# One core's transformer block in float32: rotary parts packed four heads to a tile, filling projections one unit ahead, and norms kept with tokens on the partitions

## The reference

```python
q_c, kv_c, k_rope, gq, gk, gv, gr, glow, gate_logits = split_columns(h @ w_in)
q = heads(rms_norm(q_c, q_norm_g) @ w_uq, MLA_HEADS)        # 384 -> 8 heads of 64 + 32
kv = heads(rms_norm(kv_c, kv_norm_g) @ w_ukv, MLA_HEADS)    # 256 -> 8 heads of 64 keys, 64 values
q_rope = rope_2d(q_rope, ...)                               # rotation of the 32 rope columns
p = jax.nn.softmax(s.astype(jnp.float32) * MLA_SCALE, axis=-1)
...
y = rms_norm(o, norm_g).reshape(...) * jax.nn.silu(r)       # gated heads: 4 of 128, two directions
```

## Time and profile before

| | us |
|---|---|
| median of 3 runs | 3150.24 (3149.42 to 3150.46) |
| the profiled execution: its time | 3147.42 |
| its span | 3145.4 |
| mean granted clock of TensorE | 0.986 |

### The profile page before, as it was taken

One profiled execution on the slowest core, in us unless ns is written; L12 is line 12 of the kernel. 1 busy time (PEld: TensorE's weight loads), 2 busy tenths in 40 slices (PEclk: granted clock), 3 DMA queues, 4 the chain that ended last, 5 costly groups with the idle time before them and its releaser, 6 DMA issues.

```text
span 3145.4 us, 38638 instructions
## 1 busy us (share of the span) xinstructions
PE 3038.9 (97%) x13632; PEld 2471.6 (79%) x13632; DVE 1431.6 (46%) x1871; ACT 681.5 (22%) x1187; POOL 2066.3 (66%) x2056
## 2 busy tenths in 40 slices
PE   5889999999999999999999999999999999999998
PEld 3767668778887788888888888888888887888886
DVE  7877852276456664222325322255422246542222
ACT  3244651111002542111122111100211115421110
POOL 4622217666666677777767777777777776777774
PEclk8989999999999999999999999999999999999999
DMA  6611112222222232232322222222222322332221
GB/s 257 246 41 37 34 54 94 94 81 99 96 97 91 94 102 99 94 100 94 107 87 90 98 94 100 94 97 97 94 100 94 100 94 94 101 100 95 97 97 67
DMA packets 86026, 306.73 MB, mean 98 GB/s; under 512 B 9552, under 2 KB 10064, under 8 KB 85648
## 3 DMA queue, kind: packets, MB, share of 16 engines
q1 hardware_dynamic: 82512, 297.73, 28.0%
q10 hardware_dynamic: 3392, 7.28, 0.7%
HBM read 302.87 MB, written 2.10 MB: 97 GB/s over the span
## 4 chain that ended last, share of the span: by engine, by line
PE 90%; DVE 7%; ACT 2%; issue 1%; SPq 1%; DMA 1%; DVEq 0%; ACTq 0%
PE acc L1576 85%; PE acc L725 1%; DVE rec_rec_x L1999 1%; PE side L752 1%; DVE ada_more L1152 1%; DMA xc<-in_ctx 1%; SPq L531 1%; PE side L735 0%; PE side L1576 0%; PE acc L647 0%; PE stat L1639 0%; DVE n_scaled L1129 0%; PE acc L632 0%; DVE rec_rec_x L1997 0%; DVE att_stat L1347 0%
## 5 line engine op out<-in xcount | busy, mean ns | idle before, releaser
L1538 POOL TENSOR_TENSOR w_lo<-w_raw,w_hi 128x512 fp32r<-128x512 f32 x513 | 671.8, 1310 | 1011.2 <-PE acc L1576 982.9
L1576 PE MATMUL acc<-h_hi,w_hi 128*128 128x512 f32 x2224 | 876.2, 394 | 28.7 <-ACT gq L868 11.6
L1576 PE MATMUL acc<-h_lo,w_hi 128*128 128x512 f32 x2224 | 868.5, 391 | 0.0
L1576 PE MATMUL acc<-h_hi,w_lo 128*128 128x512 f32 x2224 | 868.4, 390 | 0.0
L1539 POOL TENSOR_TENSOR w_lo<-w_raw,w_hi 128x512 fp32r<-128x512 f32 x513 | 709.4, 1383 | 0.0
L1576 PEld LDWEIGHTS acc<-h_hi,w_hi 128*128 128x128 f32 x2224 | 418.9, 188 | 130.2 <-issue 16.8
L1576 PEld LDWEIGHTS acc<-h_lo,w_hi 128*128 128x128 f32 x2224 | 419.5, 189 | 85.5 <-issue 1.9
L1576 PEld LDWEIGHTS acc<-h_hi,w_lo 128*128 128x128 f32 x2224 | 419.4, 189 | 85.2
L1527 POOL TENSOR_SCALAR w_hi<-w_raw 128x512 fp32r<-128x512 f32 x513 | 403.7, 787 | 37.1 <-DMA w_raw<-in_weights 37.1
L1968 DVE TENSOR_TENSOR x<-acc,x 128x512 f32 (+1 forms) x160 | 110.7, 692 | 661.8 <-PE acc L1576 661.7
L1576 PE MATMUL acc<-mlp_hid_hi,w_hi 128*128 128x512 f32 x1024 | 398.3, 389 | 0.0
(11 more groups left out here) (347 smaller groups left out, 3543.4 us busy)
## 6 DMA issues: line engine op xcount, KB each, us to landing
w_raw<-in_weights SPq DMA_DIRECT2D x513, 512.0 KB, 3.3
ada<-in_ada SPq DMA_DIRECT2D x36, 512.0 KB, 5.7
ada_more<-in_ada SPq DMA_DIRECT2D x10, 512.0 KB, 18.2
x<-in_x ACTq DMA_DIRECT2D x16, 256.0 KB, 6.6
out<-x SPq DMA_DIRECT2D x8, 256.0 KB, 2.2
cvec<-in_cvec ACTq DMA_DIRECT2D x1, 1024.0 KB, 5.8
ada_n<-in_ada SPq DMA_DIRECT2D x2, 512.0 KB, 17.3
xc<-in_ctx SPq DMA_DIRECT2D x1, 1024.0 KB, 16.7
```

Of the source, the lines that this page charges most:

```text
L1538: pool.tensor_tensor(w_lo[:, slot, 0:half], w_raw[:, slot, 0:half], w_hi[:, slot, 0:half].bitcast(F32), ALU.subtract)
L1576: ins = pe.matmul(out, lhs, rhs, start=start, stop=stop, skip_group_check=group)
```

## The change

- GLA_FILL and gla_order: k of head 1 is projected before unit 0; every later k and q moves one unit forward; unit 5 has no filling projection. gla_output is now an entry of the order.
- Low-rank norms: the sums of squares are products of 24 tiles of low_square (as stationary operand) with one column of ones, so tokens lie on the partitions and a sum is one column. ACT's roots and DVE's reciprocal work on 128x4 and 128x10. The query norm is not applied to z_q: it goes into the softmax scale (score_scale), which exps and probs read as a column instead of a constant. The key norm is spread back over the partitions by ACT (six scaled copies of the identity, key_diagonal) and PE (keys: a ones product of 512 and 256 columns), and DVE scales z_kv by it (low_rank_keys) after the last unit.
- Gated heads: sum is four products of one column; DVE inverts 128x4 (head_inverses); ACT makes four scaled copies of the identity (head_diagonal); PE's new output spread multiplies them by ones; head_output reads that bank. head_output stands one unit later than before.
- Query projections: the rope columns of four heads share a tile, so two outputs hold the rope rows and two their partners, then four outputs hold the 64 plain rows of two heads each. DVE turns a group of four heads with three 128x512 operations. ACT copies the turned rows of heads 0 to 3 into q_t, DVE those of heads 4 to 7. A table rope_q (512 KB) is loaded by a DMA that ACT issues after unit 7.

```diff
-GLA_FILL = [("k", 1, 2), ("q", 1, 1), ("k", 2, 2), ("q", 2, 1), ("k", 3, 2), ("q", 3, 1), ("r", 2, 1), ("r", 3, 1)]
+GLA_FILL = [("q", 1, 1), ("k", 2, 2), ("q", 2, 1), ("k", 3, 2), ("q", 3, 1), None, ("r", 2, 1), ("r", 3, 1)]
 def gla_order():
-    order = [("gate", 0, 2), ("k", 0, 2), ("gate", 1, 2)]
+    order = [("gate", 0, 2), ("k", 0, 2), ("gate", 1, 2), ("k", 1, 2)]
     for u in range(GLA_STEPS):
         order += [("turned", u, 2), ("intra", u, 1), ("added", u, 1)]
         if u % 2 == 0 and u:
             order.append(("sum", u // 2 - 1, 1))
+        if u % 2 == 1 and u > 1:
+            order.append(("spread", u // 2 - 1, 1))
+        if u == GLA_STEPS - 1:
+            order.append(("keys", 0, 2))
         if u + 2 < GLA_STEPS:
             order.append(("gate", u + 2, 2))
-        order.append(GLA_FILL[u])
+        if GLA_FILL[u]:
+            order.append(GLA_FILL[u])
+        order.append(("output", u, 0))
...
+        key_spread = norms[:, 3:5, :].rearrange("p n t -> p (n t)")
+        q_rope = [square[:, 0, :], rstd]
...
+            def token_sums(tiles, n, at):
+
                 out = begin_out()
+                for b in range(n):
+                    for k in range(tiles):
+                        ins = pe.matmul(out[:, b:b + 1], low_square[:, at(k, b):at(k, b) + P], ones[:, 0:1],
+                                        start=(k == 0), stop=(k == tiles - 1))
                 ins.then_inc(out_made, 1)
+            token_sums(QL, 4, lambda k, b: T * k + P * b)
+            token_sums(KVL, 4, lambda k, b: QL * T + TC * k + P * b)
+            token_sums(KVL, KB - 4, lambda k, b: QL * T + TC * k + T + P * b)
...
                 if name == "sum":
                     pe.wait_ge(gla_sq, i + 1)
                     out = begin_out()
+                    for b in range(4):
+                        ins = pe.matmul(out[:, b:b + 1], square[:, i % 2, P * b:P * b + P], ones[:, 0:1], start=True, stop=True)
+                    ins.then_inc(out_made, 1)
+                if name == "spread":
+                    pe.wait_ge(head_diag, i + 1)
+                    out = begin_out()
                     pe.matmul(out[:, :], ones[:, :], square[:, i % 2, :], start=True, stop=True).then_inc(out_made, 1)
+                if name == "keys":
+                    pe.wait_ge(key_diag, 1)
+                    for c0, c1 in ((0, T), (T, TC)):
+                        out = begin_out()
+                        pe.matmul(out[:, 0:c1 - c0], ones[:, :], key_spread[:, c0:c1], start=True, stop=True)\
+                          .then_inc(out_made, 1)
...
+            gla_part("spread", GH - 1)
             slot, _ = next_tile()
...
             def head_root(h):
-                if h:
-                    act.wait_ge(gla_y, h)
-                take(OUT_GLA["sum", h], root[:, :], func=ACT.Sqrt, bias=col("eps"), scale=1.0 / P)
+                take(OUT_GLA["sum", h], head_rstd[:, 0, :], func=ACT.Sqrt, bias=col("eps"), scale=1.0 / P, width=4)
                 load_exp_ln()
+            def head_diagonal(h):
+
+                act.wait_ge(head_inverse, h + 1)
+                for b in range(4):
+                    ins = act.activation(square[:, h % 2, P * b:P * b + P], identity[:, :], ACT.Copy, scale=head_rstd[:, 1, b:b + 1])
+                ins.then_inc(head_diag, 1)
+            def key_diagonal():
+                act.wait_ge(low_inverse, 1)
+                for b in range(KB):
+                    ins = act.activation(key_spread[:, P * b:P * b + P], identity[:, :], ACT.Copy, scale=low_rstd[:, 4 + b:5 + b])
+                ins.then_inc(key_diag, 1)
...
+                if d == 0 and h:
+                    head_diagonal(h - 1)
+                if u == GLA_STEPS - 2:
+                    key_diagonal()
+                    for k in range(QL):
+                        act.activation(zq_hi[k], z_q[:, k, :], ACT.Copy, scale=col("q_norm", k)).then_inc(lr_hi, 1)
                 if d == 1 and h:
                     head_output_high(h - 1)
-                if u == GLA_STEPS - 2:
-                    act.wait_ge(lr_scaled, 2)
-                    for k in range(QL):
-                        act.activation(zq_hi[k], z_q[:, k, :], ACT.Copy).then_inc(lr_hi, 1)
+            wait_taken(act, OUT_GLA["intra", GLA_STEPS - 1])
+            act.dma_start(rope_q[:, :, :], io["rope_q"]).then_inc(rope_in, 16)
...
-            for h in range(HEADS):
-                wait_made(act, OUT_QH + h)
-                act.activation(q_t[0:64, h, :], bank(OUT_QH + h)[0:64, :], ACT.Copy).then_inc(q_copied, 1)
+            for half in range(2):
+                for pair in (2 * half, 2 * half + 1):
+                    o = OUT_QH + 4 + pair
+                    wait_made(act, o)
+                    act.activation(q_t[0:64, 2 * pair, :], bank(o)[0:64, :], ACT.Copy)
+                    act.activation(q_t[0:64, 2 * pair + 1, :], bank(o)[64:P, :], ACT.Copy).then_inc(out_taken[o % BANKS], 1)
+                if half == 0:
+                    act.wait_ge(q_turned, 1)
+                    for j in range(4):
+                        act.activation(q_t[64:96, j, :], q_rope[0][32 * j:32 * j + 32, :], ACT.Copy)
             head_root(GH - 1)
...
+            head_diagonal(GH - 1)
             for tb in range(KB):
                 take(OUT_V + tb, v_mla[:, tb, :])
...
-                    act.activation(prob[:, u % 2, c0:c1], bank(o + i)[:, 0:c1 - c0], ACT.Exp, scale=MLA_SCALE,
+                    act.activation(prob[:, u % 2, c0:c1], bank(o + i)[:, 0:c1 - c0], ACT.Exp, scale=score_scale[:, 0, qb:qb + 1],
...
-                link(dve.reciprocal(square[:, 0, :], square[:, 0, :]))
-                link(dve.reciprocal(square[:, 1, 0:C], square[:, 1, 0:C]))
...
+                own(dve.reciprocal(low_rstd[:, :], low_rstd[:, :]), low_inverse, 1)
+                dve.tensor_scalar(score_scale[:, 0, :], low_rstd[:, 0:4], MLA_SCALE, None, ALU.mult)
+                link(dve.tensor_scalar(score_scale[:, 1, :], low_rstd[:, 0:4], -MLA_SCALE, None, ALU.mult))
...
+            def head_inverses(h):
+
+                wait_taken(dve, OUT_GLA["sum", h])
+                if h:
+                    dve.wait_ge(head_diag, h)
+                own(dve.reciprocal(head_rstd[:, 1, :], head_rstd[:, 0, :]), head_inverse, h + 1)
...
+                take(dve.scalar_tensor_tensor(out=o_norm[:, :], in0=gr[:, h % 2, :], scalar=col("gla_norm"),
+                                              in1=bank(o), op0=ALU.mult, op1=ALU.mult), o)
+                own(dve.tensor_tensor(o_norm[:, :], side[:, h % 2, :], o_norm[:, :], ALU.mult), gla_y, h + 1)
...
-                link(dve.tensor_tensor(square[64:96, 0, :], b[96:P, :], rope[96:P, :], ALU.mult))
-                link(dve.tensor_tensor(q_t[64:96, h, :], b[64:96, :], rope[64:96, :], ALU.mult))
-                dve.wait_ge(q_copied, h + 1)
-                take(dve.tensor_tensor(q_t[64:96, h, :], q_t[64:96, h, :], square[64:96, 0, :], ALU.add), o)
-            wait_made(dve, OUT_KH - 1)
+                take(dve.tensor_tensor(turned, bank(o), rope_q[:, 0, :], ALU.mult), o)
+                wait_made(dve, o + 1)
+                take(dve.tensor_tensor(square_sum[:, :], bank(o + 1), rope_q[:, 1, :], ALU.mult), o + 1)
+                own(dve.tensor_tensor(turned, turned, square_sum[:, :], ALU.add), q_turned, group + 1)
+            wait_made(dve, OUT_QH + HEADS - 1)
+            for j in range(4):
+                dve.tensor_copy(q_t[64:96, 4 + j, :], q_rope[1][32 * j:32 * j + 32, :])
```

More of the change, by code:

```diff
@@ L123 @@
 OUT_KH = OUT_QH + HEADS + 1
-OUT_V = OUT_KH + HEADS
+OUT_GLA["spread", GH - 1] = OUT_KH + HEADS
+OUT_V = OUT_KH + HEADS + 1
 OUT_ATT = OUT_V + KB
@@ L391, in build @@
                 decay_w = fa("decay_w", [P, GH * P])
+                with nc.sbuf_tensor("rope_q", [P, 2, T], F32) as rope_q:
+                    pass
                 intra_mask = fa("intra_mask", [P, 2, P])
@@ L694, in first_block_pe @@
             for name, i, _ in gla_order():
-                gla_part(name, i)
-                if (name, i) in [part[:2] for part in GLA_FILL]:
-                    gla_output([part[:2] for part in GLA_FILL].index((name, i)))
+                if name == "output":
+                    gla_output(i)
+                else:
+                    gla_part(name, i)
             assert turn.out == OUT_QH
@@ L913, in first_block_act @@
                 take(OUT_GV + tb, v_tok[:, tb, :])
-            take(OUT_QNORM, square_sum[:, :], func=ACT.Sqrt, bias=col("eps"), scale=1.0 / (QL * P))
-            take(OUT_KVNORM, square[:, 0, :], func=ACT.Sqrt, bias=col("eps"), scale=1.0 / (KVL * P))
-            take(OUT_KVNORM + 1, square[:, 1, 0:C], func=ACT.Sqrt, bias=col("eps"), scale=1.0 / (KVL * P), width=C)
+            take(OUT_QNORM, low_rstd[:, 0:4], func=ACT.Sqrt, bias=col("eps"), scale=1.0 / (QL * P), width=4)
+            take(OUT_KVNORM, low_rstd[:, 4:8], func=ACT.Sqrt, bias=col("eps"), scale=1.0 / (KVL * P), width=4)
```

(34 more changed lines are left out.)

81 lines of the change are left out of this document (38 added, 43 removed).

## The result

| | before | after |
|---|---|---|
| median, us | 3149.42 (3147.97 to 3150.52, 7 runs) | 3161.59 (3160.65 to 3163.65, 7 runs) |
| ratio to before | | 1.0041, 95% interval 1.0031 to 1.0050 |
| the profiled execution: its time | 3147.42 | 3161.65 |
| its span | 3145.4 | 3159.6 |
| mean granted clock | 0.986 | 0.984 |

The forecast was 3141.0, in a range of 3131 to 3148, with a chance of 0.04 for slower.

What follows compares the result with a forecast made beforehand. PE was taken to idle before the first scores, mostly waiting for DVE. Waits 19.9 + clock 7.1 - PE work 4.8 - new waits 9.9 - new clock loss 3.1 = 9.2 us saved: 3141.0 us, range 3131 to 3148.

Steps and rivals of the forecast that it cites:

- What bounds the kernel: Between token sums and first scores PE idles 19.9 us, mostly waiting for DVE; the change was to remove these waits.
- The frame: Work after the first scores is not reordered, so gains persist; a rest differing by over 2 us would disprove it.
- Theory 1: Formed after the result, not forecast: the 32-byte address shift costs 5.3 us outside the stage and a little in it.
- The clock term: Before the first scores: 7.1 us of low clock behind pauses saved, 3.1 us lost behind two new long waits.
- rival B: Narrow token sums drop PE to 1.2 GHz, taking 10.4 instead of 5.2 us; 2.0 saved, 3148 us; chance 0.12.
- What PE gets to do: PE's added work in the stage totals 4.8 us, with one-column products at 0.216 us each.
- Rival D: One-column products cost as much as 512-column ones, 0.86 us each; 16.6 us slower, 3167 us; chance 0.04.
- The new waits: Four new PE waits, at unit 5, unit 7, the key projections and spread(3), sum to 9.9 us.
- Unit 7: PE waits 3.3 us ahead of added(7) for ACT's copies of the transposes.
- Key pairs: At the key projections PE waits 1.5 us for ACT: second pair 0.3, third 1.2.
- Unit 5 to 6: Unit 5 has no filling projection, so PE waits 1.9 us for DVE around the transposes and intra.
- Edits costed at nothing: The rope_q DMA, softmax scale as a column and DVE's rope-row copies were each taken to add no time.

Runs made afterwards that it cites:

- all repairs: Kernel with both repairs plus both engines' orders, VectorE copying rotated halves of heads 0 to 3, last head's diagonals before last key copies: 3133.09 us.
- the kernel before is moved: Kernel before with eight more unused filler floats, so the first block's tensors start 32 bytes later: 3156.72 us, ratio 1.0024.
- wide sums: Changed kernel with 128 columns of ones instead of one in the token sums and heads' sums: 3153.97 us, ratio 1.0017.
- aligned kernel: Changed kernel with its three small tensors as slices of one, so later tensors stand where they stood before: 3154.80 us, ratio 1.0019.
- both repairs: Changed kernel with later tensors back at their old addresses and 128 columns of ones in token and heads' sums: 3147.68 us, ratio 0.9996.
- ScalarE's order: Changed kernel with ScalarE copying the last unit's transposes before the key diagonals and z_q's high halves: 3155.00 us, ratio 1.0020.
- VectorE's new order: Changed kernel with VectorE's head_output of units 3 and 5 before the next unit's decayed keys and queries: 3158.52 us, ratio 1.0029.

## Why the prediction was wrong, step by step

**What bounds the kernel** held: PE's idle time in the stage was 19.9 us, mostly DVE's doing, and taking the reciprocals away freed DVE. The version with all repairs shows that there was at least as much to be had: its stage is 15.4 us shorter than before (180.1 and 195.5), where 9.2 were forecast. It has two orders and an end of the stage that the forecast change had not.

**The frame failed first.** "What follows ... is not reordered, so a microsecond won before the first scores should still be there at the end", and a difference of over 2 us in the rest would prove it wrong: from the first maximum to the end it is 8.1, of which 5.3 are the addresses, 0.7 the column as scale and 1.65 a fall of the clock. The step missed is in the change itself: three tensors that stand ahead of others in memory. That their sizes add up to that of the filler they replace holds in floats but not after rounding to 32 bytes. Theory 1 is shown from both sides: merge and feed-forward lose 5.3 us when the kernel before is moved and win back 4.5 when the changed one is moved back (4.2 with the wide sums). The whole times move by more, 8.2 and 6.8 us, and that excess is clock in part and else not explained.

**The clock term had the wrong sign.** I took 7.1 as saved and 3.1 as new; measured is 14.6 in place of the 3.1. The 11.5 between are 9.7 around one-column products and 2.2 behind the wait that I didn't have; behind the two long waits that I did have it was 2.8, near the 3.1. So most of the difference is rival B, to which I gave 0.12. Its mechanism is shown; its size was 7.2 us for the token sums alone. There the products took 6.63 us and not the 10.4 of the rival, since the clock held for the first of them (20 records in 2.00 us from 162 us, 0.20 each), and 4.7 us were lost up to the second gate (15.4 with wide sums, 20.1 with narrow ones; 18.5 in the aligned kernel, where the clock fell later). With the heads' sums, which the rival left out, wide sums win 7.6 by the medians. My argument against it, that PE had been full for 30 us, was no reason: the clock was 1.00 when the sums began and fell within 5 us of them. The 1.6 us taken for the clock behind a wait of over 3 us lies within what was seen, but is no constant: 1.6 and 1.2 in the changed kernel, 2.7 at unit 7 in the one with both repairs, and none at the last diagonals in the run with ScalarE's order.

**What PE gets to do** was right: 0.20 to 0.245 us for a one-column product at full clock (10 in 2.00 us; four of L692 in 0.98) against 0.216. Rival D is out: the kernel is slower, but not by the price of the column.

**The new waits.** Unit 7: 3.4 measured, 3.3 forecast. spread(3): 3.1 and 3.2. Key pairs: 1.0 + 0.5, and 1.5 forecast. Unit 5 to 6: 1.3 and 1.9. The diagonals: four in 1.16 us and six in 1.75, 0.29 each (their own durations overlap), and I had 0.30. What failed is the list: I looked for late banks at unit 5, which has no filling, and not at unit 3, whose key projection takes spread(0)'s bank; 3.7 us.

**Edits costed at nothing.** "The softmax scale as a column lengthens ACT's instruction, but ACT waits in attention" was wrong by 0.7 us, and right in the main: ACT's exponentials of 512 columns alone grew by 3.1 us. That the 0.7 come where a unit's exponentials lie on the way to its turned probabilities is my reading and not shown.

By the forecast's own terms: 9.2 saved, less 11.5 of clock, less 3.3 of waits (13.2 idle against 9.9), is 5.6 lost in the stage; 5.3 of addresses, 2.35 in attention (0.7 of it the column as scale, 1.65 clock), 0.4 ahead of the stage and 0.4 in the other layers make 14.1 of the 14.2 between the profiles.

## What to carry to other kernels

Count a narrow product's price in clock and not in its own time: if the trace shows PE busy but the granted clock below 1.00 behind it, widen it to columns that nobody reads and look again. Where a change adds or resizes a tensor, compare the addresses of the operands that later stages stream, before any theory on their time: work that was not edited and got slower by one constant per product points there. A wait of 3.4 us was worth from 5.1 to 6.1 here, with the half clock behind it, so the order of the small copies at the end of a stage deserves the same care as the large products.

## What was not expected of the hardware

- A 128x128 by 512 product in this kernel starts every 0.2267 us when its moving operand lies at a multiple of 128 bytes, 0.2289 at 64 past and 0.2333 at 32 past. In the first block alone that is 5.3 us at 32 past.
- A stream of one-column products lets the granted clock go from 1.00 to 0.50 with PE busy throughout (164 to 172 us); the same products with 128 columns hold it at 1.00 and take less time (5.36 against 6.63 us).
- A wait of 1.2 us ahead of k(3) still had it run 10.0 to 10.2 us instead of 8.6, in all four kernels with VectorE's new order, and behind 3.7 us with wide sums it ran 10.2 as well. Behind 1.7 us before no such fall was seen, nor behind 3.1 us in the run with ScalarE's order. The length of a pause alone does not tell.
